# Score products with alternating row halves, a divided sum in the last expert pair, and a router product with its weights stationary

## The chip, the cores and the metric

The kernel runs on one core of a Trainium2 chip. The metric is the time of one execution on the device in microseconds (us). A core has a matrix engine (PE in the profile: an array of 128 rows by 128 columns that holds a stationary operand while a moving operand streams through), a vector engine (DVE), an activation engine (ACT), GpSimd (POOL) and an engine that here only issues transfers (SP). PE writes into eight PSUM banks. A float32 matmul is carried out as two PE instructions; this text calls each a pass.

## What is computed

Two blocks in a row on 256 tokens of width 1024. The first has two layers, each a mixer of three branches and a mixture of 64 experts (8 chosen of 64 for each token, hidden width 256), the second two layers of a hybrid. The parts that the change touches, cut from the reference:

```python
def diff_attention(...):      # first block, branch a
    s = jnp.einsum('bqhmd,bkhmd->bhmqk', qb, k).astype(jnp.float32) * scale    # m = 2, d = 64

def stick_breaking(...):      # first block, branch c
    z = jnp.einsum('bqhd,bkhd->bhqk', qb, k).astype(jnp.float32) * scale       # 8 heads, d = 64

def moe_ffn(u, w_router, ...):
    scores = jax.nn.sigmoid((xf @ w_router).astype(jnp.float32))               # 256 x 1024 @ 1024 x 64
    ...                                                     # choose 8 of 64, gather tokens by expert
    out = swiglu(xpad[toks], w1[e], w3[e], w2[e])
    routed = jax.ops.segment_sum(y.reshape(n_slots, D), slot_tok, num_segments=T + 1)[:T]
    shared = swiglu(xf, ws1, ws3, ws2)
    return (routed + shared).reshape(B, S, D)

for l in range(DEPTH):        # first block
    h = rms_norm(x, norm_mix_g[l]) * (1.0 + sc_m) + sh_m
    x = x + g_m * mixer(h, ...)
    h = rms_norm(x, norm_ffn_g[l]) * (1.0 + sc_f) + sh_f
    x = x + g_f * moe_ffn(h, ...)
```

The modulation vectors (sh_m, sc_m, g_m and so on) are products of one condition vector with `w_mod[l]`. The second block has a causal attention of four heads of 64 (`moba_attention`) whose scores are of the same shape of product.

## The kernel before

The order of every engine's instructions is written out by hand, with semaphores between the engines. PSUM banks are dealt out in the order of a list of product groups (`_groups_1`, `bank_plan`): `begin(name)` waits until the bank's last reader is done. Weights come through a ring of four slots, filled by SP in the order of a list of chunks; a slot is filled again when PE has released it.

Score products. Heads are 64 wide, so a head's keys and queries lie on 64 of the 128 partitions, `part` 0 to 63 or 64 to 127. For stick-breaking (L1016, z0, and L1023, z1) PE takes first all products of the lower row half, two to a bank, then all of the upper: 8 products of 256 columns (16 passes), then 8 of 128 columns (16 passes). The scores of the differential attention are built alike (L1073, s1; L1080, s0). Both stand once in each of the two layers of the first block. The second block has half of such a block in each layer (L2442, sb1 and sb0): 4 products of 256 columns, 4 of 128, again the lower half ahead of the upper.

Router (L1165). The normalized, transposed tokens `h_t` (8 chunks of 128 channels by 256 tokens) are the stationary operand, the weights `w_rt` (128 by 64 of each chunk) the moving one: 16 matmuls, 32 passes of 64 columns. Then, in layer 0 alone, PE makes part 15 of the modulation for the next layer (`mod("rt")`: L932 and L950). Then come the products of the shared expert (`shared_h`, L1173) and the counting of the chosen experts (L1209). ACT takes the router's sigmoid (L1549) and then copies part 15 (L1427). DVE chooses the experts, the last step being L1961.

Experts. They are worked off in pairs of two blocks of 64 slots: `pair_h` (L1275, the two blocks on the two column halves of PE), ACT and DVE make the gated activation (`sig_h`), `pair_turn` turns it (L1285), ACT moves the turned block out (L1582), `pair_w2` (L1296) multiplies by w2, DVE and ACT scale the result and split it in two parts (`o_parts`, L2098, L1590, L2103), and `pair_add` (L1323) sums the parts of the pair before into the tokens' banks. The parts of the very last pair are summed by `last_add` (L1310). In both layers the last turn has one pair. DVE then adds the banks to the residual (L2152, four times), the next layer's norm follows and PE turns the normalized tokens (L912). After layer 1 there is a barrier ahead of the second block; the loads of that block's first weights are issued by SP ahead of it (L438).

## Time and profile before

| | us |
|---|---|
| median of 3 runs | 2066.93 |
| lowest, highest | 2063.01, 2068.24 |
| the profiled execution | 2074.39 |
| its span, first to last instruction | 2072.6 |
| PE busy in it | 2004.1 (97%) |
| DVE busy | 986.2 (48%) |
| ACT busy | 391.2 (19%) |

The profiled execution is 7.46 us (0.4%) longer than the median; 1.8 us of its own time lie outside the span. A row of the trace gives the start of a group of like instructions, the time from its first start to its last end, engine, line, operation, the operands, shape and count; what stands in brackets is the time that the engine sat idle before, and who released it. Rows overlap on PE since its instructions are pipelined: the price of a group is the distance to the start of the next group.

### The profile page before, as it was taken

What the parts mean: (1) busy time and instruction counts of PE and PEld (TensorE: products, weight loads), DVE (VectorE), ACT (ScalarE), POOL (GpSimd) and SP (SyncE); (2) the same over time, 40 slices, a digit from 0 to 9 for tenths busy, and PEclk for the clock granted to TensorE, in tenths of its full rate; (3) what the DMA queues carried; (4) which work ended last, traced back from release to release, by engine and by line L of the source; (5) the groups of instructions that cost most, each with busy time, mean ns of one, the idle gap of its engine ahead of it and who ended that gap; (6) DMA issues with size and microseconds to landing.
All of it is one profiled execution on the core that took longest, in us unless ns stands there. A gap on an engine that the chain in (4) does not pass through costs nothing. (4 is left out here: it accounts for less than half of the span.)

```text
span 2072.6 us, 26393 instructions
## 1 busy us (share of the span) xinstructions
PE 2004.1 (97%) x9244; PEld 1188.4 (57%) x9244; DVE 986.2 (48%) x2174; ACT 391.2 (19%) x761; POOL 53.3 (3%) x134
## 2 busy tenths in 40 slices
PE   5999999999999999999999999999999997998998
PEld 3847884545444454476588655455454543484485
DVE  2887534444444444469764244444444443352351
ACT  2133111111111111123231011111111112141131
POOL 1000002000000000000000010000000001010000
PEclk9999999999999999999999989999999999999998
DMA  9655539699999999775464549999999997243420
GB/s 349 206 203 188 203 122 348 271 422 422 422 422 422 422 422 422 320 255 185 163 238 168 216 155 390 420 417 418 416 419 417 418 416 237 98 132 92 164 102 21
DMA packets 148130, 598.03 MB, mean 289 GB/s; under 512 B 13036, under 2 KB 17760, under 8 KB 96608
## 3 DMA queue, kind: packets, MB, share of 16 engines
q1 hardware_dynamic: 146656, 594.06, 73.3%
q0 software_dynamic: 1408, 3.10, 0.6%
q8 instruction: 40, 0.66, 0.1%
q14 instruction: 26, 0.21, 0.0%
HBM read 596.07 MB, written 1.05 MB: 288 GB/s over the span
## 5 line engine op out<-in xcount | busy, mean ns | idle before, releaser
L1275 PE MATMUL banks<-weight_ring,x_units 128*64 128x512 f32 x2112 | 464.9, 593 | 0.0
L1275 PEld LDWEIGHTS banks<-weight_ring,x_units 128*64 128x64 f32 x2112 | 158.3, 137 | 293.9 <-issue 293.6
L2067 DVE TENSOR_TENSOR sig_h<-banks,sig_h 128x256 f32<-128x256 f32 x66 | 28.0, 425 | 336.2 <-ACT sig_h L1577 336.2
L961 PE MATMUL banks<-h_t,weight_ring 128*128 128x256 f32 x768 | 170.1, 380 | 0.0
L961 PEld LDWEIGHTS banks<-h_t,weight_ring 128*128 128x128 f32 x768 | 145.6, 190 | 21.0 <-issue 1.6
L1250 PE MATMUL banks<-turn_hot,xn_high 128*128 128x256 f32 x544 | 139.7, 295 | 0.3 <-DVEq L2038 0.3
L2060 DVE TENSOR_SCALAR x_units<-banks,mod_col 128x256 f32<-128x256 f32 x272 | 129.5, 538 | 20.6 <-issue 14.7
L2346 PE MATMUL banks<-weight_ring,h_t 128*128 128x512 f32 (+2 forms) x384 | 135.0, 512 | 1.1 <-DMA weight_ring<-in_w_in 1.1
L1323 PE MATMUL banks<-o_parts,slot_of 128*128 128x512 f32 x512 | 133.8, 404 | 0.0
L1250 PEld LDWEIGHTS banks<-turn_hot,xn_high 128*128 128x128 f32 x544 | 102.5, 188 | 52.9 <-issue 52.7
L1250 PE MATMUL banks<-turn_hot,xn_low 128*128 128x256 f32 x544 | 131.8, 281 | 0.0
L1296 PE MATMUL banks<-slots,conv 128*64 128x512 f32 x544 | 124.3, 598 | 3.1 <-DVE x_units L2060 3.1
L901 PE MATMUL banks<-h_t,weight_ring 128*128 128x256 f32 x512 | 113.4, 385 | 3.7 <-DVEq L1643 3.7
L1296 PE MATMUL banks<-h_t,conv 128*64 128x512 f32 x256 | 116.7, 599 | 0.0
L1296 PE MATMUL banks<-qk,conv 128*64 128x512 f32 x256 | 116.7, 599 | 0.0
L883 PE MATMUL banks<-weight_ring,h_t 128*128 128x512 f32 x256 | 110.7, 593 | 0.0
L901 PEld LDWEIGHTS banks<-h_t,weight_ring 128*128 128x128 f32 x512 | 98.6, 193 | 18.3 <-issue 4.9
L2098 DVE SCALAR_TENSOR_TENSOR conv<-banks,slot_weight,gate 128x512 f32<-128x512 f32 x66 | 49.6, 752 | 117.6 <-PE banks L1296 117.6
L2346 PEld LDWEIGHTS banks<-weight_ring,h_t 128*128 128x128 f32 x384 | 69.5, 192 | 62.0 <-issue 59.1
L1250 PEld LDWEIGHTS banks<-turn_hot,xn_low 128*128 128x128 f32 x544 | 102.9, 189 | 0.5 <-issue 0.5
L1697 DVE SCALAR_TENSOR_TENSOR conv<-hpad,vec_t,conv 128x256 f32<-128x256 f32 x240 | 100.3, 480 | 5.0 <-issue 0.4
L1323 PEld LDWEIGHTS banks<-o_parts,slot_of 128*128 128x128 f32 x512 | 92.2, 190 | 16.6
(490 smaller groups left out, 2317.9 us busy)
## 6 DMA issues: line engine op xcount, KB each, us to landing
weight_ring<-in_w SPq DMA_DIRECT2D x264, 1024.0 KB, 12.2
weight_ring<-in_w_in SPq DMA_DIRECT2D x36, 2048.0 KB, 10.3
slots<-in_w SPq DMA_DIRECT2D x68, 1024.0 KB, 11.3
weight_ring<-in_w_mod SPq DMA_DIRECT2D x24, 2048.0 KB, 12.4
qk<-in_w SPq DMA_DIRECT2D x32, 1024.0 KB, 8.8
h_t<-in_w SPq DMA_DIRECT2D x32, 1024.0 KB, 10.9
weight_ring<-in_w_out SPq DMA_DIRECT2D x8, 2048.0 KB, 7.9
weight_ring<-in_w_in SPq DMA_DIRECT2D x10, 1024.0 KB, 12.3
```

What stands on the lines that cost most here:

```text
L883: mm = nc.tensor.matmul(bank[:, 0:cols], stationary[:, k, t * P:(t + 1) * P], w[:, k, 0:cols], start=(k == 0), stop=(k == KT - 1))
L901: mm = nc.tensor.matmul(bank[:, j * SEQ:(j + 1) * SEQ], w[:, k, c * P:(c + 1) * P], K.h_t[:, k, :], start=(k == 0), stop=(k == KT - 1))
L961: mm = nc.tensor.matmul(bank[:, j * SEQ:(j + 1) * SEQ], w[:, k, c * P:(c + 1) * P], K.h_t[:, k, :], start=(k == 0), stop=(k == KT - 1))
L1250: mm = nc.tensor.matmul(x_banks[q % 2][:, u * PAIRS * P:(u + 1) * PAIRS * P], xn_part(t, c, 2 * q + u), turn_hot[:, t, :], start=(t == 0 a ...
L1275: mm = nc.tensor.matmul(h_bank[own, :], x_blk[:, i, k, own], w13(2 * i + b)[:, :, k, :], start=(k == 0), stop=(k == KT - 1), skip_group_ch ...
L1296: mm = nc.tensor.matmul(o_banks[h][b * SLOTS:(b + 1) * SLOTS, :], turned[:, i, f, b * SLOTS:(b + 1) * SLOTS], w2_slots[2 * i + b][:, f, h ...
L1323: nc.tensor.matmul(y_bank[t][h][:], slot_of[:, i % PAIRS, t * P:(t + 1) * P], o_parts[:, c, h * CHUNK:(h + 1) * CHUNK], start=False, stop= ...
L1697: v.scalar_tensor_tensor(conv[:, c, :], hpad[:, c, k:k + SEQ], w, conv[:, c, :], ALU.mult, ALU.add)
L2060: last = v.tensor_scalar(out, x_banks[q % 2][:, u * PAIRS * P:(u + 1) * PAIRS * P].rearrange("p (i s) -> p i s", i=PAIRS), mod_col[:, 3, k ...
L2067: v.tensor_tensor(act_pair, h_bank[:, 0:FF], sig_pair, ALU.mult)
L2098: v.scalar_tensor_tensor(o_gated[h], o_banks[h][:], own, gate[:, 1, h * CHUNK:(h + 1) * CHUNK], ALU.mult, ALU.mult).then_inc(o_gated_ready, 1)
L2346: mm = nc.tensor.matmul(bank[:, 0:cols], stationary[:, k, t * P:(t + 1) * P], w[:, k, 0:cols], start=(k == 0), stop=(k == KT - 1))
```

## The change

- The four score blocks of the first block and the two of the second take the row halves in turn: product by product the lower half, then the upper. The waits for two banks stand ahead of the first product of the two.
- In the last pair of a layer, the sum of the pair before is divided by halves of the output's width: the first half ahead of `pair_turn`, the second behind it. `last_add` goes by output half first and token half second, and reports a token half when its second output half is in.
- The router has its weights stationary. The 8 chunks go in turn into the two column halves of PE, 64 columns each, with `h_t` (256 columns) as the moving operand, so that the even and the odd chunks are summed apart, turned, on the two halves of one bank (`rt_halves`). ACT copies this out (into `sig_g`); behind `mod("rt")` two matmuls with `ident_half` as the moving operand turn it back and add the two halves. ACT's sigmoid comes behind its copy of part 15. The list of banks has one group more, so the banks behind it shift by one.

```diff
@@ bank groups
-        + ... + mod_groups("turned", layer) + ["rt"] + mod_groups("rt", layer)
+        + ... + mod_groups("turned", layer) + ["rt_halves"] + mod_groups("rt", layer) + ["rt"]
@@ PE, stick-breaking scores (s1/s0 and sb1/sb0 are rewritten in the same way)
-                for par in range(2):
-                    part = slice(64 * par, 64 * par + 64)
-                    for i in range(2):
-                        bank = begin(("z0", par, i), l)
-                        for j in range(2):
-                            c = 2 * i + j
-                            mm = nc.tensor.matmul(bank[:, j * SEQ:(j + 1) * SEQ], kc_t[part, c, 0:P], qc_t[part, c, :],
+                for i in range(2):
+                    banks = [begin(("z0", par, i), l) for par in range(2)]
+                    for j in range(2):
+                        c = 2 * i + j
+                        for par, part in enumerate(row_half):
+                            mm = nc.tensor.matmul(banks[par][:, j * SEQ:(j + 1) * SEQ], kc_t[part, c, 0:P], qc_t[part, c, :],
                                                   start=True, stop=True)
...
+                banks = [begin(("z1", par), l) for par in range(2)]
+                for c in range(CT):
+                    for par, part in enumerate(row_half):
+                        mm = nc.tensor.matmul(banks[par][:, c * P:(c + 1) * P], kc_t[part, c, P:SEQ], qc_t[part, c, P:SEQ],
@@ PE, router
+                bank = begin("rt_halves", l)
+                for k in range(KT):
+                    wait_ht(1, l, k)
+                    half = slice(64 * (k % 2), 64 * (k % 2) + 64)
+                    mm = nc.tensor.matmul(bank[half, 0:SEQ], w_rt[:, k, :], K.h_t[:, k, :], start=(k < 2), stop=(k >= KT - 2),
+                                          skip_group_check=True)
+                mm.then_inc(B[l]["rt_halves"].full, 1)
+                mod("rt")
+
+                pe.wait_ge(rt_moved.sem, rt_moved.at(l))
                 bank = begin("rt", l)
                 for t in range(T):
-                    for k in range(KT):
-                        if t == 0:
-                            wait_ht(1, l, k)
-                        mm = nc.tensor.matmul(bank[:, t * N_EXPERTS:(t + 1) * N_EXPERTS], K.h_t[:, k, t * P:(t + 1) * P],
-                                              w_rt[:, k, :], start=(k == 0), stop=(k == KT - 1))
+                    mm = nc.tensor.matmul(bank[:, t * N_EXPERTS:(t + 1) * N_EXPERTS], rt_halves[:, t * P:(t + 1) * P], K.ident_half[:],
+                                          start=True, stop=True)
                 mm.then_inc(B[l]["rt"].full, 1)
-                mod("rt")
@@ PE, last_add
-                    for t in range(T):
-                        for h in range(2):
-                            if t == 0:
-                                pe.wait_ge(o_ready, nth(last_turn, 2 * second + h))
...
-                        mm.then_inc(y_done.sem, 1)
+                    for h, t in ((0, 0), (0, 1), (1, 0), (1, 1)):
+                        if t == 0:
+                            pe.wait_ge(o_ready, nth(last_turn, 2 * second + h))
...
+                        if h == 1:
+                            mm.then_inc(y_done.sem, 1)
@@ PE, pair
+                    if last:
+                        pair_add(it, i - 1, (0,))
                     pair_turn(it, i, last)
...
-                        pair_add(it, i - 1)
+                        pair_add(it, i - 1, (1,) if last else (0, 1))
@@ ACT
+                bank = full_of("rt_halves", l)
+                copy_out("rt_halves", l, rt_halves, bank[:, 0:SEQ])
+                act.drain().then_inc(rt_moved.sem, 1)
+                if following:
+                    copy_mod(15)
                 bank = full_of("rt", l)
                 nc.scalar.activation(score[:], bank[:, 0:T * N_EXPERTS].rearrange("p (t n) -> p t n", t=T), ACT.Sigmoid)\
...
-                if following:
-                    copy_mod(15)
```

PE's order at the stick-breaking scores of layer 0, before: the first product of each bank, and the products behind it in the two last banks (behind each row of 256 columns one more product of the same bank stands, without a wait). `slots` is the room that holds the turned keys and queries here.

```order
L1016 MATMUL banks<-slots 128x256 [waits bank7_free,qkc_t_ready]
L1016 MATMUL banks<-slots 128x256 [waits bank0_free]
L1016 MATMUL banks<-slots 128x256 [waits bank1_free]
L1016 MATMUL banks<-slots 128x256 [waits bank2_free]
L1023 MATMUL banks<-slots 128x128 [waits bank3_free]
L1023 MATMUL banks<-slots 128x128 x3
L1023 MATMUL banks<-slots 128x128 [waits bank4_free]
```

The same place on PE in the changed kernel:

```order
L1017 MATMUL banks<-slots 128x256 [waits bank1_free,bank7_free,qkc_t_ready]
L1017 MATMUL banks<-slots 128x256 x3
L1017 MATMUL banks<-slots 128x256 [waits bank2_free,bank0_free]
L1024 MATMUL banks<-slots 128x128 [waits bank4_free,bank3_free]
L1024 MATMUL banks<-slots 128x128 x7
```

Before, banks 7 and 0 belong to the lower row half and are filled first; now bank 7 (lower) and bank 1 (upper) are asked for together and filled product by product in turn.

PE's order around the router of layer 0, before, from the first product to the shared expert:

```order
L1165 MATMUL banks<-w_rt,h_t 128x64 [waits ht_ready1_dve,bank2_free,other_params_loaded]
L1165 MATMUL banks<-w_rt,h_t 128x64 x9
L932 MATMUL banks<-weight_ring,c_act 32x512 [waits bank3_free,slot2_filled]
L950 MATMUL banks<-act_h,part_share 64x512 [waits bank0_free,bank4_free]
L950 MATMUL banks<-act_t,part_share 64x512 [waits bank3_free]
L1173 MATMUL banks<-weight_ring,h_t 128x512 [waits bank1_free,bank0_free,bank2_free,bank7_free,slot3_filled,bank6_free,bank5_free]
```

And in the changed kernel (`ident_half` is the two identities of 64 on the two partition halves, `sig_g` holds the copied halves):

```order
L1166 MATMUL banks<-h_t,w_rt 64x256 [waits ht_ready1_dve,bank2_free,other_params_loaded]
L1166 MATMUL banks<-h_t,w_rt 64x256 [waits ht_ready1_act]
L933 MATMUL banks<-weight_ring,c_act 32x512 [waits bank3_free,slot2_filled]
L951 MATMUL banks<-act_h,part_share 64x512 [waits bank0_free,bank4_free]
L951 MATMUL banks<-act_t,part_share 64x512 [waits bank3_free]
L1174 MATMUL banks<-ident_half,sig_g 128x64 [waits bank5_free,rt_halves_moved]
L1181 MATMUL banks<-weight_ring,h_t 128x512 [waits bank2_free,bank1_free,bank3_free,bank0_free,slot3_filled,bank7_free,bank6_free]
```

The router's sum now ends behind part 15 of the modulation, with two small products that wait for ACT's copy. In layer 1, where there is no part 15, these two follow the first eight directly.

PE's order in the last pair, before:

```order
L1285 MATMUL banks<-ident,sig_h 128x128 [waits pair_act_ready]
L1285 MATMUL banks<-ident,sig_h 128x128
L1320 REGISTER_ALU [waits pair_slot_of_ready]
L1323 MATMUL banks<-o_parts,slot_of 128x512 [waits half_o_ready]
L1323 MATMUL banks<-o_parts,slot_of 128x512 x3
L1296 MATMUL banks<-slots,conv 64x512 [waits w2_slot1_filled,w2_slot0_filled]
```

And in the changed kernel:

```order
L1331 MATMUL banks<-o_parts,slot_of 128x512 [waits half_o_ready]
L1331 MATMUL banks<-o_parts,slot_of 128x512 x3
L1293 MATMUL banks<-ident,sig_h 128x128 [waits pair_act_ready]
L1331 MATMUL banks<-o_parts,slot_of 128x512 [waits half_o_ready,pair_slot_of_ready]
L1304 MATMUL banks<-slots,conv 64x512 [waits w2_slot1_filled,w2_slot0_filled]
```

Four of the eight summing products (one instruction each) now stand ahead of the turning of the last activation, four behind it.

## Rows read from the trace of the kernel before

**Rows 1.** The page, busy time of the engines.

```profile
PE 2004.1 (97%) x9244; PEld 1188.4 (57%) x9244; DVE 986.2 (48%) x2174; ACT 391.2 (19%) x761; POOL 53.3 (3%) x134
```

**Rows 2.** Timeline of PE, stick-breaking scores, layer 0: start, us, what, count, idle before.

```profile
97.63 2.32 PE L1016 MATMUL banks<-slots 64*128 64x256 f32 x13 [0.72 <-ACTq L1463]
...
99.79 0.38 PE L1016 MATMUL banks<-slots 64*128 64x256 f32 x1
99.80 0.38 PE L1023 MATMUL banks<-slots 64*128 64x128 f32 x2
100.01 0.38 PE L1016 MATMUL banks<-slots 64*128 64x256 f32 x1
...
101.42 0.70 PE L883 MATMUL banks<-weight_ring,h_t 128*128 128x512 f32 x1
```

**Rows 3.** Timeline of PE, second block's scores, layer 0, and the work behind.

```profile
1833.93 1.68 PE L2442 MATMUL banks<-bqk_t 64*128 64x256 f32 x16
1835.54 0.70 PE L2373 MATMUL banks<-h_t,weight_ring 128*128 128x256 f32 x2
```

**Rows 4.** Timeline of PE, router of layer 0 to the shared expert.

```profile
348.19 3.79 PE L1165 MATMUL banks<-w_rt,h_t 128*128 128x64 f32 x32
351.90 1.92 PE L932 MATMUL banks<-weight_ring,c_act 128*32 128x512 f32 x16
353.75 1.07 PE L950 MATMUL banks<-act_h,part_share 128*64 128x512 f32 x2
...
355.54 0.70 PE L1173 MATMUL banks<-weight_ring,h_t 128*128 128x512 f32 x1
```

**Rows 5.** Shared expert's weights issued at 341.7 to 342.5, KB, median us to landing.

```profile
weight_ring<-in_ws SPq DMA_DIRECT2D x2, 1024.0 KB, 10.3
```

**Rows 6.** Timelines of DVE and PE: the choice, and its reader, layer 0.

```profile
361.76 0.42 DVE L1961 TENSOR_TENSOR chosen<-rest,biased 128x256 f32<-128x256 f32 x1
...
369.38 0.33 PE L1209 MATMUL banks<-chosen,strict 128*128 128x64 f32 x2
```

**Rows 7.** Timeline of PE, router of layer 1 and the shared expert.

```profile
1198.92 7.06 PE L1165 MATMUL banks<-w_rt,h_t 128*128 128x64 f32 x32
1205.78 16.52 PE L1173 MATMUL banks<-weight_ring,h_t 128*128 128x512 f32 x32
```

**Rows 8.** Stretches: length, busy PE, PEld, DVE, ACT, POOL, granted clock, DMA, GB/s.

```profile
1198.90:1205.80 6.90, 6.90 (x34) 6.90 (x33) 0.97 (x2) 2.64 (x4) 6.75 (x4) 0.50 0.08 33
```

**Rows 9.** Timelines of PE, ACT and DVE, last expert pair of layer 0.

```profile
876.70 0.51 PE L1285 MATMUL banks<-ident,sig_h 128*128 128x128 f32 x2 [1.45 <-DVE sig_h L2069]
876.97 2.09 PE L1323 MATMUL banks<-o_parts,slot_of 128*128 128x512 f32 x8
878.99 3.65 PE L1296 MATMUL banks<-slots,conv 128*64 128x512 f32 x16
884.09 2.44 PE L1310 MATMUL banks<-o_parts,slot_of 128*128 128x512 f32 x8 [1.45 <-DVE o_parts L2103]
...
877.25 0.38 ACT L1582 ACTIVATE conv<-banks 128x256 f32<-128x256 f32 x1 [1.56 <-PE banks L1285]
...
885.65 2.71 DVE L2152 TENSOR_TENSOR x_tokens<-x_tokens,banks 128x512 f32<-128x512 f32 x4 [0.48 <-PE banks L1310]
```

**Rows 10.** Timelines of SP and DVE at the end of layer 1.

```profile
1728.45 14.90 SPq L438 DMA_DIRECT2D weight_ring<-in_w_in  x5
...
1738.81 2.71 DVE L2152 TENSOR_TENSOR x_tokens<-x_tokens,banks 128x512 f32<-128x512 f32 x4 [0.83 <-PE banks L1310]
```

**Rows 11.** The page, costliest groups: busy, mean ns of one, idle before.

```profile
L1275 PE MATMUL banks<-weight_ring,x_units 128*64 128x512 f32 x2112 | 464.9, 593 | 0.0
L1275 PEld LDWEIGHTS banks<-weight_ring,x_units 128*64 128x64 f32 x2112 | 158.3, 137 | 293.9 <-issue 293.6
```

**Rows 12.** An issue of expert weights at 1276.3 to 1276.6, and PE's next start.

```profile
weight_ring<-in_w SPq DMA_DIRECT2D x1, 1024.0 KB, 7.2
...
1283.68 1.05 PE L1275 MATMUL banks<-weight_ring,x_units 128*64 128x512 f32 x4
```

More of the change, by code:

```diff
@@ L391, in _groups_1 @@
         + [("wo", h, t) for t in range(T) for h in range(2)] + mod_groups("wo", layer)
-        + [("xT", 1, g) for g in range(4)] + mod_groups("turned", layer) + ["rt"] + mod_groups("rt", layer)
+        + [("xT", 1, g) for g in range(4)] + mod_groups("turned", layer) + ["rt_halves"] + mod_groups("rt", layer) + ["rt"]
         + [("=moe_y", t, h) for t in range(T) for h in range(2)] + ["-moe_h", "-moe_x"] + [("-moe_o", h) for h in range(2)]
@@ L617, in first_block @@
         merged_ready = signal("merged_ready", 4)
-        score_ready, chosen_ready = signal("score_ready"), signal("chosen_ready")
+        score_ready, chosen_ready, rt_moved = signal("score_ready"), signal("chosen_ready"), signal("rt_halves_moved")
+        rt_halves = sig_g[:, 0, 0:SEQ]
         sh_h_done, sh_sig_ready, sh_act_ready, sh_turned, sh_act_t_ready, sh_done = (
@@ L1067, in _ @@
                 pe.wait_ge(qkt_ready.sem, qkt_ready.at(l))
-                for m in range(2):
-                    part = slice(64 * m, 64 * m + 64)
-                    for i in range(2):
-                        bank = begin(("s1", m, i), l)
-                        for j in range(2):
-                            mm = nc.tensor.matmul(bank[:, j * SEQ:(j + 1) * SEQ], qa_t[part, 2 * i + j, P:SEQ],
-                                                  ka_t[part, 2 * i + j, :], start=True, stop=True)
-                        mm.then_inc(B[l]["s1", m, i].full, 1)
-                for m in range(2):
-                    part = slice(64 * m, 64 * m + 64)
-                    bank = begin(("s0", m), l)
-                    for h in range(DA_HEADS):
-                        mm = nc.tensor.matmul(bank[:, h * P:(h + 1) * P], qa_t[part, h, 0:P], ka_t[part, h, 0:P],
+                for i in range(2):
+                    banks = [begin(("s1", m, i), l) for m in range(2)]
+                    for j in range(2):
+                        for m, part in enumerate(row_half):
+                            mm = nc.tensor.matmul(banks[m][:, j * SEQ:(j + 1) * SEQ], qa_t[part, 2 * i + j, P:SEQ],
+                                                  ka_t[part, 2 * i + j, :], start=True, stop=True)
+                            if j == 1:
+                                mm.then_inc(B[l]["s1", m, i].full, 1)
+                banks = [begin(("s0", m), l) for m in range(2)]
+                for h in range(DA_HEADS):
+                    for m, part in enumerate(row_half):
+                        mm = nc.tensor.matmul(banks[m][:, h * P:(h + 1) * P], qa_t[part, h, 0:P], ka_t[part, h, 0:P],
                                               start=True, stop=True)
-                    mm.then_inc(B[l]["s0", m].full, 1)
+                        if h == DA_HEADS - 1:
+                            mm.then_inc(B[l]["s0", m].full, 1)
                 for h in range(2):
@@ L2437, in _ @@
                 for n, q0, keys in (("sb1", P, SEQ), ("sb0", 0, P)):
-                    for par in range(2):
-                        part = slice(64 * par, 64 * par + 64)
-                        bank = begin((n, par), l)
-                        for i in range(2):
-                            mm = nc.tensor.matmul(bank[:, i * keys:(i + 1) * keys], bqk_t[part, 0, i, q0:q0 + P],
+                    banks = [begin((n, par), l) for par in range(2)]
+                    for i in range(2):
+                        for par in range(2):
+                            part = slice(64 * par, 64 * par + 64)
+                            mm = nc.tensor.matmul(banks[par][:, i * keys:(i + 1) * keys], bqk_t[part, 0, i, q0:q0 + P],
                                                   bqk_t[part, 1, i, 0:keys], start=True, stop=True)
-                        mm.then_inc(B[n, par].full, 1)
+                            if i == 1:
+                                mm.then_inc(B[n, par].full, 1)
                 by_columns("t1", ("c_c", "g_b"))
```

24 lines of the change are left out of this document (11 added, 13 removed).

## The prediction, made before the changed kernel ran

> **What bounds the kernel now.** I read the page's busy times first: PE works 97% of the span, DVE under half of it [rows 1]. So the time is PE's instructions plus a few waits, and an edit is worth what it takes from PE's own line, unless a transfer or another engine comes last at that place. Next I read PE's timeline at each edited place, and take distances from start to start, not durations, because pipelined rows overlap. In the expert stage PE never waits for weights (idle 0.0 ahead of L1275, [rows 11]); but the cover there is thin: in layer 1 a load issued at 1276.3 to 1276.6 lands 7.2 later, and the products that need it start at 1283.68 [rows 12]. That comes back as a rival.
>
> **Scores of the first block.** The block runs from 97.63 to 101.42, 3.79 us [rows 2]; the three others like it (L1073 with L1080, and the same in layer 1) I take as equal. At 99.79 and 99.80 an upper-half product of 256 columns and a lower-half one of 128 start 10 ns apart: the halves do run together, and out of written order, but only where PE reaches a product of the other half soon enough. Products of one half start 0.215 apart (99.79, 100.01). In the second block the same products, half as many (8 passes of 256 columns and 8 of 128), take 1.61 (1833.93 to 1835.54) [rows 3]. That is the price if both halves run together from the first pass: 4 x 0.2155 + 4 x b + start = 1.61. The first block has 16 + 16 passes; I read its course as 4 passes alone, 8 in pairs with the next bank, 4 paired with those of 128 columns, and the last 4 + 4 of 128 columns partly alone, which is 12 steps of 256 and 8 of 128: 12 x 0.2155 + 8b + start = 3.79. The two give b = 0.114 and start = 0.29. With strict alternation nothing is alone: 8 x 0.2155 + 8 x 0.114 + 0.29 = 2.93. Gain 0.86 a block, **3.45 for four**. In the second block the halves already run together; gain 0. The bounds: 0 (if alternation brings PE nothing more) to 4 x 1.0. The wait for two banks ahead of the first product costs nothing as far as I see: PE's only wait at that place is the 0.72 for ACT's copy [rows 2], the banks' older readers are copies ahead of that one. Work that reads the scores waits longer than this for PE elsewhere, so PE's line is what moves.
>
> A rule speaks against this. The Trainium skill, "TensorE: Matmul & The Clock Gate", section "The mechanism" of Part 3, says that matmuls start and end strictly in program order. The trace disagrees: in [rows 2] a product of L1023 starts while products of L1016, which stand ahead of it, have yet to start (100.01). By the rule the block before would have been longer than it is, and the one after one step of 0.2155 longer than 2.93, so 2.6 in place of 3.45 for four; I stay with the rows.
>
> **Last pair, layer 0.** Behind the last L1275, PE sits idle for 1.45 until the activation is ready (876.70), then does the turning, eight summing instructions (876.97 to 878.99, 2.02 or about 0.23 each with a first one of 0.3) and w2 [rows 9]. Four of the eight move into the idle time: 4 x 0.23 = 0.93, which fits in 1.45. What is late next is ACT's move of the turned block: 877.25 + 0.38 = 877.63 [rows 9], and w2 would start at 878.99 - 0.93 = 878.06, so it doesn't wait. What follows (o_parts, L1310, L2152, the norm, L912) waits for one another in a chain, so the gain is passed on, less the new order in `last_add`: token half 0 is done after the sixth instruction instead of the fourth; two of these six now stand in the time in which PE waited for the second output half, so it costs 0 to 0.23, and I take 0.13. **Gain 0.80**, bounds 0.5 to 1.0.
>
> **Last pair, layer 1.** The same on PE, but behind it is a barrier. SP's issues of the next weights last from 1728.45 to 1743.35 whatever PE does here, while DVE's last addition ends at 1738.81 + 2.71 = 1741.52 [rows 10]. SP is 1.8 late against it. **Gain 0**, bounds 0 to 0.8.
>
> **Router, layer 0.** Before: 348.19 to 351.90, 3.71 for 32 passes, 0.116 each [rows 4]. After: 16 passes of 256 columns in two column halves. That the two column halves run side by side is what L1275 does (two blocks on column halves; 16 passes of L932 on four column quarters take 351.90 to 353.75, 1.85, which is 4 steps of 0.43 and 0.13 of start [rows 4]). So 8 x 0.2155 + 0.15 = 1.87, gain 1.84. The two products that turn back and add: 4 passes of 64 columns at 0.116 plus a start of 0.13 = 0.59. ACT's copy is hidden behind part 15 (351.90 to 355.54): it needs some 0.4 (0.38 for a copy of the same size, [rows 9]). **Gain 1.25**, bounds -0.5 (column halves one after the other) to 1.4. Two covers get thinner. The shared expert's two loads are issued from 341.7 on and take 10.3 at the median [rows 5], so they are in by about 353; L1173 would start at 355.54 - 1.25 = 354.3, which fits, though not by much. The choice (L1961) is ready at 362.18, its reader at 369.38 [rows 6]; the sigmoid now comes behind part 15, some 3 us later, the reader 1.25 earlier: 7.2 - 4.3 = 2.9 are left.
>
> **Router, layer 1.** Here PE's clock is low: granted 0.50 in the stretch of the router [rows 8], that is the 1.2 GHz level, and the router takes 1198.92 to 1205.78 = 6.86 in place of 3.71 [rows 7]. There is no part 15 to hide the turn-round. After, at the same clock: 8 x 0.431 + 0.1 = 3.55; then PE waits for its last pass to end, ACT's copy and its drain, 0.2 + 0.38 + 0.14 = 0.72; then 4 x 0.213 = 0.85. Sum 5.12, **gain 1.75**. Were the clock full there, it would be 1.87 + 0.72 + 0.59 = 3.18 against 3.71, a gain of 0.5.
>
> **Sum.** 3.45 + 0.80 + 1.25 + 1.75 = 7.25 us off the profiled execution's 2074.39, so 2067.1. That execution was 0.36% above the median of the runs; taken off the median, 2066.93 - 7.25 = **2059.7**. Changes within 0.3% (6.2 us, about what a measurement of this kernel can tell from no change) end at 2060.7, so the forecast lies just beyond.
>
> **Rivals.**
> 1. *The clock comes back sooner in layer 1.* The shared expert there takes 16.52 with a slow start [rows 7] against 369.38 - 355.54 = 13.84 in layer 0 [rows 4, 6]. The router's products now fill both column halves, and if the clock is full when the shared expert starts, some 2.6 more go, with up to 1 in the router: about 3.3, time 2056.4. Against it: the new wait of 0.72 for ACT, and that the clock is granted by what PE did before, which the trace shows only for the old order.
> 2. *The weight stream takes layer 1's gain.* Loads land a few tenths ahead of PE there [rows 12]. If the stream kept its own time, PE's 2 x 0.86 + 1.75 = 3.5 of layer 1 would turn into waits at L1275: 2063.2. Against it: SP issues a load when PE frees its slot, so the stream starts with PE.
> 3. *Column halves don't hide their weight loads.* If each pair of passes in the router waited for two loads of 0.137 [rows 11], it would cost 8 x 0.274 = 2.2 in layer 0 and twice that at the low clock in layer 1: -7.25 + 6.6, so 2066.3. The idle 0.0 ahead of L1275, with the same shapes, speaks against it. It is what the Trainium skill, same page and section, gives as a rule (loads overlap with running matmuls only in other rows of the array); by that rule the trace disagrees.
> 4. *Slower: alternation parts the halves.* If PE finds no second product to run beside the first when they alternate, every pass stands alone: a first-block score block becomes 16 x 0.2155 + 16 x 0.114 + 0.29 = 5.56 (+1.77), a second-block one 2.93 (+1.32), so +9.7 for six in place of -3.45: 2066.93 + 9.7 - 3.8 = 2072.8. It decides from +0.65 a block on, where it eats the other 3.8. Against it: [rows 3], where PE finds the other half four passes away.
> 5. *The scores don't gain*, since PE's look-ahead already did what can be done: -3.8, 2063.1.
>
> **How the numbers follow.** Forecast 0.52, rival 1 0.22, rival 2 0.09, rival 3 0.04, rival 4 0.05, rival 5 0.08. The forecast's own bounds: 4.8 to 9 us off, 2058 to 2062. The range takes in rivals 1, 2 and 5 with a little for the scatter of the median (before's runs lie 5 us apart): 2054 to 2064.5, leaving out rivals 3 and 4 and the tails. Faster by over 0.3%: 0.68 of the forecast (0.35), 0.95 of rival 1 (0.21), a tenth of rivals 2 and 5 (0.02), together 0.58. Slower: most of rival 4, 0.04. Within: 0.38.
>
> **What would show it.** Right: the four score blocks at 2.9, the second block's at 1.6; the router of layer 0 at 1.9 with two products of 0.6 behind part 15; in layer 1 a wait of about 0.7 ahead of those two, the stretch to the shared expert at 5.1; in the last pair of layer 0 four sums in the old idle, w2 0.9 sooner after L1275. Wrong: score blocks above 3.8; new idle ahead of the shared expert or of L1209 in layer 0; idle ahead of L1275 in layer 1's expert stage; router passes of one column half that don't start with the other's.

## The result and the profile after

The changed kernel takes 2056.41 us (median of 6 runs, 2052.65 to 2059.71) against 2068.34 for the kernel before beside it: a ratio of 0.9939, 95% interval 0.9917 to 0.9960, or 12.6 us less by the ratio (11.9 by the medians). Measured again on another chip the ratio was 0.9953 (0.9936 to 0.9970), 9.7 us less (10.5 by the medians). The forecast was 7.25 us less, 2059.7, range 2054 to 2064.5; the direction held and the time lies in the range, at the value of the first rival (2056.4). That the two agree to the decimal is luck: the rival had been taken off a median of 2066.93, and it was for 10.55 less. The profiled execution of the changed kernel took 2056.76, with a span of 2055.0; that of before had 2072.6.

The busy times of the changed kernel's page, and from its costliest groups the first products of an expert pair (busy, mean ns of one, idle before):

```profile
PE 1986.5 (97%) x9220; PEld 1171.3 (57%) x9220; DVE 984.5 (48%) x2174; ACT 391.9 (19%) x763; POOL 53.4 (3%) x134
```
```profile
L1283 PE MATMUL banks<-weight_ring,x_units 128*64 128x512 f32 x2112 | 464.9, 592 | 0.0
```

PE is as full as in [rows 1], with 17.6 us less of it. There is no idle time ahead of L1283, the first products of an expert pair: the weight stream took nothing back.

The stick-breaking scores of layer 0 and the second block's scores on PE's timeline (start, us, what, count, idle before), which answer to [rows 2, 3]:

```profile
97.27 2.00 PE L1017 MATMUL banks<-slots 64*128 64x256 f32 x16 [0.72 <-ACTq L1473]
99.10 1.06 PE L1024 MATMUL banks<-slots 64*128 64x128 f32 x16
100.09 2.41 PE L884 MATMUL banks<-weight_ring,h_t 128*128 128x512 f32 x5
...
1820.93 1.58 PE L2455 MATMUL banks<-bqk_t 64*128 64x256 f32 x16
1822.43 3.94 PE L2386 MATMUL banks<-h_t,weight_ring 128*128 128x256 f32 x17
```

From start to start a first-block score block takes 100.09 - 97.27 = 2.82 (3.79 before), and the three others like it the same; the second block's takes 1.50 in each layer (1.61 and 1.62 before).

The router of layer 0, answering to [rows 4, 6], then that of layer 1, answering to [rows 7], and last the first counting product of layer 1 before:

```profile
345.79 1.90 PE L1166 MATMUL banks<-h_t,w_rt 128*64 128x256 f32 x16
347.62 1.92 PE L933 MATMUL banks<-weight_ring,c_act 128*32 128x512 f32 x16
...
351.26 0.66 PE L1174 MATMUL banks<-ident_half,sig_g 128*128 128x64 f32 x4
351.92 13.97 PE L1181 MATMUL banks<-weight_ring,h_t 128*128 128x512 f32 x32
365.73 0.33 PE L1217 MATMUL banks<-chosen,strict 128*128 128x64 f32 x2
```
```profile
1192.36 2.54 PE L1166 MATMUL banks<-h_t,w_rt 128*64 128x256 f32 x16
1195.41 0.66 PE L1174 MATMUL banks<-ident_half,sig_g 128*128 128x64 f32 x4 [0.51 <-ACTq L1560]
1195.91 13.95 PE L1181 MATMUL banks<-weight_ring,h_t 128*128 128x512 f32 x32
1209.70 0.33 PE L1217 MATMUL banks<-chosen,strict 128*128 128x64 f32 x2
```
```profile
1222.13 0.33 PE L1209 MATMUL banks<-chosen,strict 128*128 128x64 f32 x2
```

In layer 0 the router's own products went from 3.71 to 1.83, and from its first product to the first counting product (L1209, now L1217) it is 19.94 after 21.19. In layer 1 the same stretch went from 1222.13 - 1198.92 = 23.21 to 17.34, 5.87 less, and that is the largest single step. Two things make it up: from the router to the shared expert it is 1195.91 - 1192.36 = 3.55 after 6.86, 3.31 less, and the shared expert itself takes 13.79, as in layer 0, after 1222.13 - 1205.78 = 16.35, 2.56 less. The stretches of the two kernels show why (length, busy PE, PEld, DVE, ACT, POOL, granted clock, DMA share, GB/s; first the router and the start of the shared expert after, then the latter before):

```profile
1192.30:1195.40 3.10, 2.60 (x17) 1.41 (x16) 0.99 (x2) 1.79 (x4) 2.95 (x3) 0.79 0.14 58
1195.90:1202.80 6.90, 6.90 (x18) 3.11 (x18) 4.78 (x29) 1.09 (x2) 4.58 (x2) 1.00 0.00 1
```
```profile
1205.80:1210.90 5.10, 5.10 (x7) 2.11 (x7) 3.73 (x26) 0.28 (x1) 1.27 (x1) 0.50 0.00 2
```

Before, the whole router [rows 8] and the first 5.1 us of the shared expert ran at a granted clock of 0.50, the lower of the two levels (1.2 GHz). After, the clock is full (2.4 GHz) within the router: read in windows of 0.1 us, it falls 2.2 us ahead of the router's first product and rises 1.3 us behind it. Before, it falls 1.7 ahead and rises 12.1 behind.

The last pair of layer 0, answering to [rows 9]:

```profile
871.61 1.20 PE L1331 MATMUL banks<-o_parts,slot_of 128*128 128x512 f32 x4
873.12 0.51 PE L1293 MATMUL banks<-ident,sig_h 128*128 128x128 f32 x2 [0.32 <-DVE sig_h L2082]
873.39 1.18 PE L1331 MATMUL banks<-o_parts,slot_of 128*128 128x512 f32 x4
874.50 3.65 PE L1304 MATMUL banks<-slots,conv 128*64 128x512 f32 x16
879.61 2.11 PE L1317 MATMUL banks<-o_parts,slot_of 128*128 128x512 f32 x8 [1.45 <-DVE o_parts L2116]
885.30 1.16 PE L913 MATMUL banks<-ident,xn 128*128 128x128 f32 x8 [3.58 <-DVEq L1645]
```

The idle time ahead of the turning fell from 1.45 to 0.32, with four sums in its place. From the start of the last hidden product to the next layer's first turn (L912, now L913) it is 14.22 after 15.00: 0.78 less. In layer 1 SP's issues still end last:

```profile
1716.03 15.21 SPq L438 DMA_DIRECT2D weight_ring<-in_w_in  x5
```

They end at 1731.24, DVE's last addition at 1728.32. In both kernels they start 7.08 behind the first hidden product of the last pair; they took 15.21 after 14.90 [rows 10], and from the last hidden product to the second block's first turn it is 20.67 after 20.35. Nothing is gained there, as [rows 10] had told, and the 0.3 more is SP's.

### The profile page after: what moved, and what is told of

Same layout as the page of the kernel before. It is cut to its first block and busy times, and to the rows that moved or that the text cites. A ratio compares the mean times of both kernels' runs of the same rounds, so it can differ in the third digit from the quotient of the medians.

```text
span 2055.0 us, 26367 instructions
## 1 busy us (share of the span) xinstructions
PE 1986.5 (97%) x9220; PEld 1171.3 (57%) x9220; DVE 984.5 (48%) x2174; ACT 391.9 (19%) x763; POOL 53.4 (3%) x134
## 5 line engine op out<-in xcount | busy, mean ns | idle before, releaser
L1283 PE MATMUL banks<-weight_ring,x_units 128*64 128x512 f32 x2112 | 464.9, 592 | 0.0
L1283 PEld LDWEIGHTS banks<-weight_ring,x_units 128*64 128x64 f32 x2112 | 158.0, 137 | 294.2 <-issue 293.9
## 6 DMA issues: line engine op xcount, KB each, us to landing
weight_ring<-in_w SPq DMA_DIRECT2D x264, 1024.0 KB, 12.1
weight_ring<-in_w_mod SPq DMA_DIRECT2D x24, 2048.0 KB, 12.6
```

The costliest lines, as they stand in the source:

```text
L1283: mm = nc.tensor.matmul(h_bank[own, :], x_blk[:, i, k, own], w13(2 * i + b)[:, :, k, :], start=(k == 0), stop=(k == KT - 1), skip_group_ch ...
```

## The experiments

Every kernel left a profile. Of layer 1 one number is followed through all of them: the time from the router's first product to the first counting product ("the stretch").

**The scores alone** (the kernel before with only the new order of the score products):

```diff
-                for par in range(2):
-                    for i in range(2):
-                        bank = begin(("z0", par, i), l)
+                for i in range(2):
+                    banks = [begin(("z0", par, i), l) for par in range(2)]
...
+                        for par, part in enumerate(row_half):
```

> Only the score products alternate; router and last pair as before. Theory (router): the low-clock stretch of layer 1 belongs to the old router, so from the router's first product to the first counting product it stays at some 23 us (23.2 before, 17.3 in the changed kernel); each first-block score block takes 2.8 (3.79 before), the second block's 1.5 (1.61), so 4 x 0.97 + 2 x 0.11 = 4.1 us less in all. Rival (moment): the clock came back sooner because all work ahead of it had moved; then the stretch is shortened here too, to some 17 to 20, and the total is 7 to 10 less.

Measured: ratio 0.9973 (0.9959 to 0.9987), 5.6 us less. The blocks take 2.82 and 1.51. But the stretch, with the old router, is 17.63:

```profile
1193.66 3.47 PE L912 MATMUL banks<-ident,xn 128*128 128x128 f32 x16 [2.76 <-DVEq L1633]
1197.07 4.00 PE L1166 MATMUL banks<-w_rt,h_t 128*128 128x64 f32 x32
1200.91 13.95 PE L1174 MATMUL banks<-weight_ring,h_t 128*128 128x512 f32 x32
1214.70 0.33 PE L1210 MATMUL banks<-chosen,strict 128*128 128x64 f32 x2
```

So the old router can run at full clock too (1200.91 - 1197.07 = 3.84), and the theory that it always holds the low clock falls. The low stretch was there, but earlier: the clock fell 2.9 us ahead of the router's first product, while PE worked on L912, and rose 0.6 behind it.

**The last pair alone**:

```diff
+                    if last:
+                        pair_add(it, i - 1, (0,))
                     pair_turn(it, i, last)
...
-                        pair_add(it, i - 1)
+                        pair_add(it, i - 1, (1,) if last else (0, 1))
...                                                            # last_add by output halves, as in the change
```

> Only the last pair's sums are divided and the last sums reordered. From the last pair's w2 products seen against its hidden products 0.85 less in both layers, 0.1 given back ahead of the next norm's turn in layer 0, nothing left in layer 1 behind the barrier: 0.7 us in all, which the time alone can't tell from 0. Rival: layer 1's gain is kept, 1.5.

Measured: ratio 0.9981 (0.9967 to 0.9995), 3.9 us less, with an interval that ends at 1.0. By the rows it is the expected 0.78 in layer 0 (14.22 after 15.00) and nothing in layer 1 (20.58 after 20.35). The old router's stretch was 17.56, and here no clock fell: from 3 us ahead of the router to its end it was full.

```profile
1198.10:1204.90 6.80, 5.91 (x49) 5.44 (x48) 2.91 (x6) 3.49 (x6) 5.26 (x3) 1.00 0.54 225
```

So this profile says nothing on which router ends a low stretch. The rows don't account for all of the time measured.

**The router alone** (the new router in both layers, the rest as before):

```diff
-                        mm = nc.tensor.matmul(bank[:, t * N_EXPERTS:(t + 1) * N_EXPERTS], K.h_t[:, k, t * P:(t + 1) * P],
-                                              w_rt[:, k, :], start=(k == 0), stop=(k == KT - 1))
+                    mm = nc.tensor.matmul(bank[half, 0:SEQ], w_rt[:, k, :], K.h_t[:, k, :], start=(k < 2), stop=(k >= KT - 2),
+                                          skip_group_check=True)
...                                                            # turning back, ACT and the bank list as in the change
```

> Only the router is changed. Theory (router): the new order of products itself ends the low clock in layer 1; router to first counting product takes some 17.3 (23.2 before), in layer 0 1.2 less, so 7.1 us less in all. Rival (moment): without the shift from the scores the clock stays low through the router; the stretch is some 21.4 and the total 3.0 less.

Measured: ratio 0.9957 (0.9943 to 0.9971), 8.9 us less; stretch 16.93; in layer 0 19.75. More than the theory's 7.1 and far more than the rival's 3.0. But the profile can't show that the new router ends a low stretch, since there was none, from 3 us ahead of the router's first product (1195.14) to the shared expert:

```profile
1192.10:1198.30 6.20, 4.79 (x37) 3.33 (x37) 2.91 (x6) 3.14 (x7) 4.61 (x3) 1.00 0.60 252
```

What agrees with the theory is the mean granted clock of its ten runs, 0.992 against 0.988 for the kernel before beside it.

**The changed kernel with the old router in layer 1**:

```diff
+                if l == 0:
+                    ...                                    # the new router
+                else:
+                    ...                                    # the old one
```

> The changed kernel with the old router in layer 1 alone. Theory (router): the stretch in layer 1 is back at some 23; total 4.1 + 0.7 + 1.2 = 6.0 us less than before. Rival (moment): the stretch is 17 to 20, total 9 to 12 less, as in the changed kernel.

Measured: ratio 0.9993 (0.9979 to 1.0008), 1.4 us less, less of a gain than either theory expected. The stretch is back at 22.80:

```profile
1193.94 7.06 PE L1184 MATMUL banks<-w_rt,h_t 128*128 128x64 f32 x32
1200.79 16.11 PE L1192 MATMUL banks<-weight_ring,h_t 128*128 128x512 f32 x32
1216.74 0.33 PE L1228 MATMUL banks<-chosen,strict 128*128 128x64 f32 x2
```

Against the changed kernel that is 5.5 in the stretch; the timed runs differ by more, and their mean granted clock was the lowest of the kernels so far (mean 0.986, before 0.988).

**The changed kernel again**, unedited, on the chip of the next three:

> The changed kernel once more, beside the next kernels on one chip. Both theories: ratio near 0.994. Theory (instructions and clock): the part of the gain that doesn't come from the clock is the four score blocks (3.9), the second block's (0.2), the router (1.2 and 0.6 at full clock), the last pair (0.7), 6.6 us; runs of before and of this at the same mean granted clock differ by 6 to 9. Rival (clock alone beyond the scores): they differ by 4.

Measured: ratio 0.9953; stretch 17.47. Each timed run comes with its mean granted clock. Over the 160 runs of all kernels for which it is on record, with a level for each kernel, the time falls by 1.55 us for each 0.001 of mean clock, and what is left scatters by 0.9 us a run. At a clock of 0.990 the kernel before stands at 2066.7, the changed one at 2057.8, scores alone at 2061.2, last pair alone at 2064.5, router alone at 2062.9, old router in layer 1 at 2061.5. So 8.9 us remain when runs of equal clock are compared, near the upper end of what was expected; and most of the low result of the kernel with the old router in layer 1 is clock: at equal clock it has 5.3 of the expected 6.0.

Not all of this is accounted for. At equal clock the scores alone give 5.5, the last pair alone 2.2, the router alone 3.8 and the whole change 8.9, where the rows at full clock give 4.1, 0.8, 1.8 and 6.6: some 1.4 to 2.3 too much in each of these four (with the old router in layer 1 it is 0.7 too little), and the three parts add up to more than the whole. A part may lie in the comparison: over 2066 us, 0.001 of mean clock is 4.1 us at half the clock, which would cost a PE that is always busy 2.1, and the fit gives 1.55. A low stretch on busy PE, like the router's, then costs more than the comparison takes off. That is an estimate and doesn't cover all of it; the rest is open.

**One column half** (the changed kernel, all eight chunks in the same 64 columns of PE):

```diff
-                    mm = nc.tensor.matmul(bank[half, 0:SEQ], w_rt[:, k, :], K.h_t[:, k, :], start=(k < 2), stop=(k >= KT - 2),
+                    mm = nc.tensor.matmul(bank[0:64, 0:SEQ], w_rt[:, k, :], K.h_t[:, k, :], start=(k == 0), stop=(k == KT - 1),
...                                                            # the copy and the turning back on 64 rows alone
```

> The changed kernel, the router's eight chunks all in the same column half. Theory: the two column halves do run side by side and hide their weight loads; taken away, the router's 16 passes of layer 0 need 16 x 0.2155 + 0.15 = 3.6 in place of 1.83, so all that the router gained in layer 0 is gone (1.7 us more than the changed kernel in each layer at full clock). Rival (loads not hidden): 16 x (0.2155 + 0.137) = 5.6.

Measured: ratio 0.9946 (0.9928 to 0.9964), which doesn't tell it from the changed kernel; at equal clock it stands at 2060.9, 3.1 above it (2 x 1.7 expected), and the rows tell it too.

```profile
348.36 3.62 PE L1165 MATMUL banks<-h_t,w_rt 128*64 128x256 f32 x16
351.91 1.92 PE L933 MATMUL banks<-weight_ring,c_act 128*32 128x512 f32 x16
...
1198.49 4.37 PE L1165 MATMUL banks<-h_t,w_rt 128*64 128x256 f32 x16
```

In layer 0 the router takes 3.55 (expected 3.6; 5.6 with loads exposed): a pass every 0.22, so even with one half the loads are hidden, and the second half brings the other factor of two (1.83). In layer 1 the clock rises 1.5 us behind the router's first product here too (stretch 19.30), so in this profile the second column half isn't what brings it back.

**Alternating by two** (the changed kernel, first-block scores in turns of two products, four passes):

```diff
-                    for j in range(2):
-                        c = 2 * i + j
-                        for par, part in enumerate(row_half):
+                    for par, part in enumerate(row_half):
+                        for j in range(2):
+                            c = 2 * i + j
...                                                            # the products of 128 columns and L1074, L1081 alike
```

> The changed kernel, the first block's score products alternating by two (four passes of one half, then four of the other). Theory: PE finds the other half four passes away, as in the second block before, so a block takes 2.8 to 3.0. Rival: it needs the other half in the next product, the block goes back towards 3.8.

Measured: ratio 0.9947 (0.9932 to 0.9962); a block takes 101.50 - 98.58 = 2.92, 0.10 above strict alternation:

```profile
98.58 2.10 PE L1017 MATMUL banks<-slots 64*128 64x256 f32 x16 [0.72 <-ACTq L1473]
...
101.50 0.70 PE L884 MATMUL banks<-weight_ring,h_t 128*128 128x512 f32 x1
```

Cut to the moment 98.60 to 98.62, the same timeline has two passes running, which started within 0.02 us of each other; passes of one half start 0.22 apart, so these are of both halves, though the other half's first pass stands behind four of this one:

```profile
98.58 0.49 PE L1017 MATMUL banks<-slots 64*128 64x256 f32 x2 [0.72 <-ACTq L1473]
```

Eight passes ahead PE didn't find the other half at once (3.79), four ahead it did. The 0.10 is the same as the second block's 1.61 against 1.51, which had been written in turns of two before.

**The turn back later** (the changed kernel, the router's two last products behind the first half of the shared expert):

```diff
-                for t in range(T):
-                    shared_h(t, w13(RING - 1))
+                shared_h(0, w13(RING - 1))
+                pe.wait_ge(rt_moved.sem, rt_moved.at(l))
+                ...                                        # the two products with ident_half
+                shared_h(1, w13(RING - 1))
```

> The changed kernel, the router's two last products behind the first half of the shared expert's. Theory: in layer 1 the wait for ACT's copy (0.51, and some 0.3 of the last pass's tail) is hidden, 0.8 us less than the changed kernel; the choice is 3.5 later against a slack of some 5, so the counting products don't wait. Rival: the choice becomes late, the counting products wait in one of the layers, no gain or a loss of up to 1.

Measured: ratio 0.9999 (0.9982 to 1.0016). The twelve runs lie in two groups, seven from 2062.89 to 2065.17 (mean granted clock 0.988 to 0.991) and five from 2073.83 to 2075.96 (0.983): by the mean all of the change's gain is gone, by the median (2064.83 against 2068.30) 3.5 us of it are left. The half of the shared expert is 16 passes of 0.43, 6.9 us and not the 3.5 of the expectation, which overdrew the slack:

```profile
368.00 0.41 PE L1216 MATMUL banks<-chosen,strict 128*128 128x64 f32 x2 [1.80 <-DVEq L1974]
...
370.46 0.51 PE L1182 MATMUL banks<-ident,act_h 128*128 128x128 f32 x2 [1.21 <-DVE act_h L1992]
```
```profile
370.00:380.00 10.00, 8.68 (x22) 4.52 (x22) 6.04 (x35) 1.15 (x3) 0.00 (x0) 0.66 0.54 224
```

PE waits 1.80 for the choice and 1.21 behind it, and the stretch that follows has a granted clock of 0.66, where the changed kernel has 1.00. From the router to the first expert pair layer 0 takes 42.85 (36.96 in the changed kernel), layer 1 37.30 (34.17): together 9.0, in a profiled execution of the first group (2064.50, against 2057.93 for the changed kernel beside it). The rival held, and its price was put too low: in layer 0 waits of 3 us cost nearly as much again in clock. What puts five runs into the second group is open.

**The kernel before, twice more**, unedited, for its profile:

> The kernel before once more, for its profile. Theory (old router holds the low clock, now and then): in layer 1 from the router's first product to the first counting product 23 or 17.6, both possible; over the three old-router kernels of this call at least one 23. Rival (chance that has nothing to do with the router): 17 to 18 in nearly all, as in the two last old-router profiles.

> The kernel before a third time, for its profile; as for the one ahead.

Stretch 21.66 and 21.68, between the two values expected and nearer the long one; the router at the low clock (6.86) in both, the shared expert partly.

```profile
1199.42 7.06 PE L1165 MATMUL banks<-w_rt,h_t 128*128 128x64 f32 x32
1206.28 14.99 PE L1173 MATMUL banks<-weight_ring,h_t 128*128 128x512 f32 x32
1221.10 0.33 PE L1209 MATMUL banks<-chosen,strict 128*128 128x64 f32 x2
```

**The old router in layer 1, again**, unedited, for its profile:

> The changed kernel with the old router in layer 1, a second time, for its profile. Its mean granted clock was the lowest of all kernels in the timed runs (0.986), so the theory (old router) expects the long stretch, 22.8, again; the rival some 17.6.

Stretch 22.84, as expected of the old router.

**Wide products ahead of the old router** (the kernel before; in layer 1 the first half of the shared expert ahead of the router):

```diff
+                shared_h(0, w13(RING - 1))
+                if l > 0:
+                    ...                                    # the old router
+                shared_h(1, w13(RING - 1))
```

> The kernel before, in layer 1 with the first half of the shared expert (512-column products) ahead of the old router. Theory (old router): the wide products bring the clock back, the old router then runs at the full clock; its products take 3.7 and the stretch from the first shared product to the counting is some 19 (6.9 + 6.9 + 3.7 and 1.7 of low clock), if the choice isn't late; mean clock of the timed runs above that of before (0.989). Rival: the low stretch is as long as before in some runs whatever stands there, mean clock as before.

Measured: ratio 1.0003 (0.9993 to 1.0012), mean granted clock 0.990 against 0.989; from the first shared product to the counting 19.52 (19 expected).

```profile
1201.75 8.85 PE L1174 MATMUL banks<-weight_ring,h_t 128*128 128x512 f32 x16 [1.58 <-ACTq L1434]
1210.44 3.68 PE L1212 MATMUL banks<-w_rt,h_t 128*128 128x64 f32 x32
1213.96 7.08 PE L1174 MATMUL banks<-weight_ring,h_t 128*128 128x512 f32 x16
1221.27 0.41 PE L1220 MATMUL banks<-chosen,strict 128*128 128x64 f32 x2 [0.23 <-DVEq L1973]
```

The old router runs at full clock here (1213.96 - 1210.44 = 3.52), behind wide products of which some ran low (8.69 for 16 passes, 6.9 at full clock). But PE waited 1.58 ahead of them for the last tokens and the choice came late, so the time stayed. One profile, and a new wait in it: it agrees with the theory and doesn't settle it.

## Why the prediction was right, and where it was off

**The stretch of layer 1, in all profiles.**

The last column goes further: from layer 1's first turning of normalized tokens ahead of the router (L912, or L913) to the second block's first (L2383, or L2396).

| router in layer 1 | stretch, us | to the second block, us |
|---|---|---|
| old: before, before again, before a third time | 23.21, 21.66, 21.68 | 552.60, 552.60, 552.75 |
| old: rest of the change in place, twice | 22.80, 22.84 | 552.42, 552.02 |
| old: scores alone, last pair alone | 17.63, 17.56 | 548.70, 547.01 |
| new: the changed kernel twice, router alone, by two | 17.34, 17.47, 16.93, 17.21 | 547.12, 547.17, 545.98, 548.13 |
| new in one column half | 19.30 | 549.27 |
| new, turned back later (0.23 of it a wait for the choice) | 17.26 | 550.28 |

The rows of the first value in the lines "before" and "changed kernel":

```profile
1195.57 1.16 PE L912 MATMUL banks<-ident,xn 128*128 128x128 f32 x8 [2.76 <-DVEq L1632]
1748.17 3.68 PE L2383 MATMUL banks<-ident,xn 128*128 128x128 f32 x16 [8.47 <-DVEq L2654]
```
```profile
1188.95 1.16 PE L913 MATMUL banks<-ident,xn 128*128 128x128 f32 x8 [2.76 <-DVEq L1645]
1736.07 3.68 PE L2396 MATMUL banks<-ident,xn 128*128 128x128 f32 x16 [10.03 <-DVEq L2668]
```

In two of the thirteen profiles, last pair alone (old router) and router alone (new), the clock did not fall near the router, so they don't bear on what ends a low stretch. In the eleven others it fell 1.4 to 2.9 us ahead of the router's first product. With the old router it then rose 8.9 to 12.1 us behind that product in 5 of 6 (0.6 in scores alone, where it had fallen earliest), with the new one 1.0 to 1.6 behind it in all 5. Were both routers alike, and the profiles independent, the five long ones would all fall to the old router about once in 77 draws. So what rival 1 said is what happens: the clock comes back within the router. The kernel with the old router put back in layer 1 alone shows the long stretch twice. Which property of the new products does it (fewer passes, a wider moving side, a shorter router) is open; rival 1's own reason, that both column halves are filled, is excluded by the one profile with one half.

For the size, the last column is the steadier measure. The kernel before loses 1.5 us less in the stretch in two of its profiles, but there the clock falls once more, 26 us behind the router's first product, and in all three it takes 552.6 to 552.8 to the second block; the changed kernel takes 547.1 and 547.2. That is 5.5 less, with the 0.3 that SP cost at the end inside it: 5.8 for the router in layer 1. The means of the stretch over mixed kernels, 21.06 for the seven with the old router and 17.24 for the four with the new one as it is, differ by 3.8; they take in the two kernels in which the old router met little or no low clock.

**Point by point.**

- *PE bounds the time.* Right: no weight stream, no late choice, no new wait but the 0.51 of layer 1, so what was taken from PE's line was kept, but for the end of layer 1, where SP comes last.
- *Scores, 3.45.* Right in mechanism; 4 x 0.97 = 3.9, and 2 x 0.10 in the second block where 0 had been taken. The start of 0.29 taken from the second block still held 0.1 for its turns of two; with 2.82 it is 0.19. The Trainium skill, "TensorE: Matmul & The Clock Gate", section "The mechanism" of Part 3, has matmuls start strictly in program order. In the run that alternates by two the trace disagrees again: at 98.58 a product of the other half starts beside the first, ahead of passes written before it.
- *Last pair, layer 0, 0.80.* Measured 0.78, and its parts hold: w2 starts 0.91 sooner behind the last hidden product (0.93 forecast), and 0.12 is given back at `last_add` (0.13). *Layer 1, 0.* Measured -0.3 to -0.2: SP's issues decide.
- *Router, layer 0, 1.25.* Measured 1.25 to 1.44. The router's 1.87 came as 1.83; the two products as 0.66 in one profile and 0.49 in others. Column halves hide their loads, as the idle 0.0 of [rows 11] said.
- *Router, layer 1, 1.75.* This is the term that was mis-sized: 5.8 (5.87 in the stretch of the two profiles). The forecast took the low clock of one profile for given on both sides. It had 5.12 from the router to the shared expert, and 3.55 came, close to the 3.18 that it had worked out for a full clock; and it had no gain in the shared expert, where 2.56 came. So this step of the working failed, and the time lies in the range because the range took in rival 1; the forecast's own bounds ended at 2058. The wait of 0.72 was right (L1166's last pass at 1194.52, L1174 at 1195.41: 0.89 with one pass of 0.22 in it).
- *Sum.* 3.9 + 0.2 + 0.8 + 1.3 - 0.3 + 5.8 = 11.7 (9.7 with the 3.8 of the mixed means), against 9.7 and 12.6 measured. So the account closes to within a few us, not to the decimal. The 17.6 between the two profiled spans is more, mostly since the first profile had a further low stretch that the second had not:

```profile
2027.00:2042.00 15.00, 13.38 (x50) 10.73 (x50) 2.21 (x5) 1.79 (x3) 0.00 (x0) 0.50 0.01 1
```

- *Rivals.* 1 came true in what it said of the clock, not in its reason. 2 is out: no idle time ahead of L1283. 3 and 4 are out by the rows of layer 0 and of the scores. 5 is out by the 3.9.
- *The choice's slack of 2.9 in layer 0.* It was more: the choice is ready at 360.04 + 0.43 = 360.47, its reader starts at 365.73, 5.3 later.

```profile
360.04 0.43 DVE L1974 TENSOR_TENSOR chosen<-rest,biased 128x256 f32<-128x256 f32 x1
```

  Counted from the router's first product the choice came 0.7 later, not 3: the sigmoid came 2.3 later, but the step of DVE that follows it took 0.29 where it had taken 1.95 before:

```profile
352.35 1.95 DVE L1921 TENSOR_TENSOR biased<-score,rt_bias 128x128 f32<-128x128 f32 x1 [2.16 <-ACTq L1551]
```
```profile
352.30 0.29 DVE L1934 TENSOR_TENSOR biased<-score,rt_bias 128x128 f32<-128x128 f32 x1 [4.40 <-ACTq L1566]
```

  Before, GpSimd worked on L864 at that moment, until 354.16, and the step ended 0.14 behind it, at 354.30. In the profiles of before again, scores alone and last pair alone it ended 0.14 to 0.15 behind GpSimd's end too, while in the changed kernel GpSimd was done at 351.84, ahead of the step. So it looks as if the step had waited for GpSimd's end; no run varies this alone. The later turn-back, 7.5 behind, spent the slack and more.

## What to carry to other kernels

Products on half the rows run beside each other if PE meets the other half soon, so write them in turns; here turns of one or two differ by 0.1 us, and eight passes apart cost 1 us a block. A product with few output columns is cheaper with that narrow side stationary, in two column halves (here 3.71 went to 1.83; in one half it was 3.55), when the turn back and its copy hide behind other work, and only as far as the reader's slack goes. Before a profile's low-clock stretch is priced as fixed, take a second profile, and measure up to a point well behind it: it may be a matter of what PE does there.

## What the runs showed of the hardware that I had not expected

- The same kernel's layer 1 stretch differed by 1.5 us between profiles (23.21, 21.66, 21.68), and by 5.6 between kernels with the same old router there (23.21 against 17.56); the granted clock is the difference that the rows show. Up to the second block the three profiles of the kernel before agree to 0.15 us, since the clock falls again in the two with the shorter stretch.
- Times of a kernel follow the mean granted clock closely: 1.55 us for each 0.001, with 0.9 us a run left over. Kernels that share most of their edits compare well at equal clock (one column half 3.1 above the changed kernel, 3.4 expected; by two 0.5, 0.4 by its rows); between the kernel before and those with one part of the change or all of it, 1.4 to 2.3 us stay unexplained.
- Waits of 1.80 and 1.21 us added in one place (the turn back later) were followed by a stretch at a granted clock of 0.66 that cost nearly as much again.
